# First layer of a two-layer trunk: head sums in column groups, roots spread from 32 rows, the mixing bias as a table, and halves of the u products between the small products

## The reference

```python
def chunk_gating(u, va, w_s, b_s):               # 8 groups of 64 columns, chunks of 128 tokens
    vc = va.reshape(b, t // CHUNK, CHUNK, A_GROUPS, A_GROUP_DIM)
    s = jnp.einsum('gpq,bnqgc->bnpgc', w_s, vc) + b_s.T[None, None, :, :, None]
    return u * s.reshape(b, t, A_WIDTH)

def even_project(h, w_in, q_gain, k_gain):
    u, va, q, k, v = jnp.split(h @ w_in, list(EV_SPLITS), axis=-1)     # 512, 512, 512, 128, 128 columns
    q = rms_norm(q.reshape(b, t, B_KV_HEADS, B_GROUP, HEAD_DIM), q_gain)   # per head of 64
    k = rms_norm(k.reshape(b, t, B_KV_HEADS, HEAD_DIM), k_gain)
# latent tokens: q = axial_rope(q, ...), k = axial_rope(k, ...), then block attention;
# out = concatenate([u * s, attention]) @ w_out; a mixture of experts follows; layer 2 likewise
```

## Time and profile before

| | |
|---|---|
| time, median of 3 runs | 1390.81 us (1388.46 to 1392.39) |
| the profiled execution | 1387.17 us, its span in the trace 1385.0 us |
| mean granted TensorE clock | 0.949 |
| PE busy | 1263.4 us, 91% of the span |
| DVE, ACT, POOL busy | 870.2, 705.5, 235.9 us |
| DMA | 324.98 MB, mean 235 GB/s |

### The profile page before, as it was taken

How to read it: one execution, slowest core, us unless ns; L and a number is a source line. 1 busy time by engine, 2 the same in 40 slices (tenths; PEclk the granted TensorE clock), 3 DMA queues, 4 the chain that set the end, 5 groups by cost and what they waited for, 6 DMA issues and landing times.

```text
span 1385.0 us, 18165 instructions
## 1 busy us (share of the span) xinstructions
PE 1263.4 (91%) x7550; PEld 911.6 (66%) x7550; DVE 870.2 (63%) x1013; ACT 705.5 (51%) x819; POOL 235.9 (17%) x133
## 2 busy tenths in 40 slices
PE   5999988899399999999789998999984999999997
PEld 2897856788266666666469984667872666666662
DVE  5613546423678888888385252553344899999994
ACT  3531146611467777777343124554123777776772
POOL 3100000011302222211030000000124033333330
PEclk9997899999699999999899999899996999999996
DMA  9710182042799999999883222002419999999974
GB/s 364 247 63 31 33 277 104 1 153 92 275 369 357 384 379 380 385 391 397 290 276 103 95 68 72 1 1 92 153 41 381 379 376 377 385 383 382 393 294 161
DMA packets 100472, 324.98 MB, mean 235 GB/s; under 512 B 6720, under 2 KB 30495, under 8 KB 84007
## 3 DMA queue, kind: packets, MB, share of 16 engines
q1 hardware_dynamic: 89376, 290.88, 55.7%
q0 software_dynamic: 8400, 27.58, 7.7%
q10 hardware_dynamic: 2614, 5.35, 1.0%
HBM read 300.29 MB, written 23.50 MB: 234 GB/s over the span
## 4 chain that ended last, share of the span: by engine, by line
PE 74%; DMA 8%; ACT 7%; DVE 6%; POOL 2%; issue 1%; SPq 0%; ACTq 0%; POOLq 0%; DVEq 0%
PE psum L944 71%; ACT arena L1814 4%; DVE arena L2270 2%; DMA stage<-in_moe_w_up 2%; DVE w_lo L2000 2%; DMA h_hi<-h_dram,arena 1%; POOL arena L891 1%; PE psum L1464 1%; DMA stage<-in_moe_w_gate 1%; DMA h_dram<-arena 1%; DMA stage<-in_w_mod 1%; DMA arena<-in_x_sample 1%; DMA arena<-in_od_w_in 1%; ACT arena L1581 1%; ACT w_hi L1890 1%
## 5 line engine op out<-in xcount | busy, mean ns | idle before, releaser
L944 PE MATMUL psum<-w_hi,h_hi 128*80 128x512 f32 (+1 forms) x848 | 330.4, 390 | 8.4 <-DVE w_lo L2000 5.0
L2000 DVE TENSOR_TENSOR w_lo<-stage,w_hi 128x2048 fp32r<-128x2048 f32 (+1 forms) x122 | 275.5, 2270 | 99.5 <-ACT w_hi L1594 59.5
L944 PE MATMUL psum<-w_lo,h_hi 128*80 128x512 f32 (+1 forms) x848 | 326.0, 384 | 0.0
L944 PE MATMUL psum<-w_hi,h_lo 128*80 128x512 f32 (+1 forms) x848 | 325.7, 384 | 0.0
L1890 ACT ACTIVATE w_hi<-stage 128x2048 fp32r<-128x2048 f32 x100 | 190.6, 1915 | 60.2 <-PE psum L944 37.0
L944 PE MATMUL psum<-h_hi,w_hi 128*128 128x320 f32 x672 | 212.4, 316 | 2.0 <-DVE h_lo L2047 2.0
L944 PE MATMUL psum<-h_lo,w_hi 128*128 128x320 f32 x672 | 209.7, 312 | 0.0
L944 PE MATMUL psum<-h_hi,w_lo 128*128 128x320 f32 x672 | 209.6, 312 | 0.0
L909 POOL DMA_INDIRECT acc_dram<-arena x31 | 120.2, 3878 | 413.0 <-ACT arena L1922 227.8
L2000 DVE TENSOR_TENSOR w_lo<-arena,w_hi 128x2048 fp32r<-128x2048 f32 x73 | 166.7, 2288 | 31.0 <-ACT w_hi L1890 28.2
L944 PEld LDWEIGHTS psum<-w_hi,h_hi 128*80 128x80 f32 (+1 forms) x848 | 129.9, 153 | 82.5 <-issue 13.7
(11 more groups left out here) (275 smaller groups left out, 1289.8 us busy)
## 6 DMA issues: line engine op xcount, KB each, us to landing
stage<-in_w_mod SPq DMA_DIRECT2D x46, 1024.0 KB, 9.0
stage<-in_moe_w_up SPq DMA_DIRECT2D x36, 1024.0 KB, 15.7
stage<-in_moe_w_down SPq DMA_DIRECT2D x34, 1024.0 KB, 15.0
stage<-in_moe_w_gate SPq DMA_DIRECT2D x30, 1024.0 KB, 15.2
arena<-in_moe_w_gate SPq DMA_DIRECT2D x29, 1024.0 KB, 16.2
arena<-in_moe_w_up SPq DMA_DIRECT2D x23, 1024.0 KB, 15.4
arena<-in_moe_w_down SPq DMA_DIRECT2D x19, 1024.0 KB, 15.5
xT<-in_moe_w_down SPq DMA_DIRECT2D x11, 1024.0 KB, 19.5
```

The costliest lines, as they stand in the source:

```text
L944: return pe.matmul(o, w, x, start=first, stop=last, skip_group_check=True)
L2000: return nc.vector.tensor_tensor(dst, src, hi.bitcast(F32), ALU.subtract)
```

## The change

On TensorE:

- `head_sums` uses two tables of 128x32 in place of five of 128x10. Tile k and q 0, q 1, q 2 write output rows 0 to 31, 32 to 63, 64 to 95, 96 to 127; q 3 adds to the rows of k with the second table. The roots then lie on all 128 partitions, two of each 32 in use. The result has new banks, 6 and 7, which hold `va 0` before, and a new product group `s bias` stands ahead of it.
- A spread reads the 32 rows of its group, table and roots, in place of 10.
- The mixing bias is made once: four products of 128x128 from the 8 rows, brought by ScalarE to a table `s_bias`. The four 8-row products of 512 columns and the four of 128 columns go. VectorE adds the table where it copied the mixing out.
- Each u product but the last is cut in two halves of 24 products along the inner axis, and the spreads, mixings and pair turns stand between the halves. `u 0` starts behind the second spread. The mixing of the context comes first of the mixings.
- The rows of modulation chunk 4 come ahead of `u 3`, those of chunk 5 behind it, and both transposes after that.

On VectorE and ScalarE the order follows: the low part of `out 0` is made after the second scaling, that of `out 1` after the third mixing; ScalarE splits the second u piece behind the roots, and `out 1` ahead of the swapped keys (which now wait for the last mixing), and brings over the rows of chunk 4 before the four gated tiles. The scratch tile of the rotation and the tables lie elsewhere, and banks are given by name in `plan_psum`.

```diff
+HEAD_GROUP, SECOND_IN_GROUP = {4: 0, 0: 1, 1: 2, 2: 3, 3: 0}, 3
...
+            one("v lat", "act"), one("v ctx", "act"), one("cache k", "act"), one("s bias", "act", in_order=False)
...
+            for name, banks in ((("qk spread", 4), (0, 1)), (("qk spread", 0), (2, 3)), (("qk spread", 1), (0, 1)), (("qk spread", 2), (2, 3)),
...
+        pick_ = small[:, 256:320]
+        pick = pick_.rearrange("p (m r) -> p m r", m=2)
+        pick_rows = arena[:, 5248:5248 + 2 * P]
+        head_var, head_root = rstd, sq[0]
+        s_bias = v3(arena, T, 4, P)
...
-                    mm(bank(name, 0)[0:10, :], pick[:, m, :], head_sq[m][:, LAT], m == 0, m == 4)
-                    ins = mm(bank(name, 1)[0:10, 0:NC], pick[:, m, :], head_sq[m][:, CTX], m == 0, m == 4)
+                    own = slice(32 * HEAD_GROUP[m], 32 * HEAD_GROUP[m] + 32)
+                    w = pick[:, int(m == SECOND_IN_GROUP), :]
+                    mm(bank(name, 0)[own, :], w, head_sq[m][:, LAT], m < 4, m != SECOND_IN_GROUP)
+                    ins = mm(bank(name, 1)[own, 0:NC], w, head_sq[m][:, CTX], m < 4, m != SECOND_IN_GROUP)
                     ins.then_inc(sq_used if m < 4 else psum_full, 1)
...
-                    for m in range(5):
-                        ins = pe.transpose(pair("pick rows", 10, 5 * P)[:, P * m:P * m + P], pick[:, m, :], ident)
-                    ins.then_inc(psum_full, 1)
+                    for g in range(4):
+                        mm(bank("pick rows")[32 * g:32 * g + 32, 0:P], pick[:, 0, :], ident, True, True)
+                    mm(bank("pick rows", 1)[0:32, 0:P], pick[:, 1, :], ident, True, True).then_inc(psum_full, 1)
...
+                    pe.wait_ge(sel_in, 16)
+                    begin("s bias")
+                    for g in range(4):
+                        ins = mm(bank("s bias")[:, P * g:P * g + P], sel[:, g, :], bs, True, True)
+                    ins.then_inc(psum_full, 1)
                     head_sums("qk norm")
...
+                    def spread_root(m):
+
+                        name, g = ("qk spread", m), 32 * HEAD_GROUP[m]
+                        at = P * int(m == SECOND_IN_GROUP)
                         begin(name)
+                        mm(bank(name, 0), pick_rows[g:g + 32, at:at + P], head_root[g:g + 32, LAT], True, True)
...
+                    def mix_latents(g):
+
                         begin(("s", g))
-                        b_rows = bs.rearrange("p (o q) -> p o q", o=1).to_broadcast([8, 4, P])
-                        mm(bank(("s", g)).rearrange("p (o q) -> p o q", o=4), sel[:, g, :], b_rows, True, False)
                         for t in range(4):
                             for j in range(2):
                                 ins = mm(bank(("s", g))[64 * j:64 * j + 64, P * t:P * t + P],
-                                         va[:, t, P * g + 64 * j:P * g + 64 * j + 64], ws_tile(2 * g + j), False, t == 3)
+                                         va[:, t, P * g + 64 * j:P * g + 64 * j + 64], ws_tile(2 * g + j), True, True)
...
+                    def project_half(m, part_of_k):
+
+                        hi, lo = weights(("u", m // 2))
+                        name, c = ("u", m), P * (m % 2)
+                        if part_of_k == 0:
+                            begin(name)
+                        for k in range(4 * part_of_k, 4 * part_of_k + 4):
+                            w = (hi[:, k, c:c + P], lo[:, k, c:c + P])
+                            for half in range(2):
+                                tk = slice(HT * half, HT * half + HT)
+                                ins = passes(bank(name, half)[:, 0:HT], w, (h_hi[:, k, tk], h_lo[:, k, tk]), k == 0, k == KD - 1)
+                        if part_of_k == 1:
+                            ins.then_inc(psum_full, 1)
+
+                    spread_root(4)
+                    spread_root(0)
+                    project_half(0, 0)
+                    spread_root(1)
+                    spread_root(2)
+                    project_half(0, 1)
+                    spread_root(3)
+                    emptied(pe, ("va", 1, 2))
+                    emptied(pe, "wsT1")
+                    mix_context()
+                    mix_latents(0)
+                    pe.wait_ge(cs_in, 16)
+                    turn_pairs(4)
+                    project_half(1, 0)
+                    turn_pairs(0)
+                    mix_latents(1)
+                    project_half(1, 1)
+                    turn_pairs(1)
+                    mix_latents(2)
+                    project_half(2, 0)
+                    turn_pairs(2)
+                    mix_latents(3)
+                    project_half(2, 1)
+                    turn_pairs(3)
                     begin("new k")
                     pe.transpose(bank("new k")[:, 0:P], kT[:, P + NL:KEYS], ident).then_inc(psum_full, 1)
-                    project(("u", 0), [("u", 1)], at=(P,))
-                    project(("u", 1), [("u", 2), ("u", 3)])
-                    modulation("qk")
+                    mod_rows(MOD_AT["qk"][0])
+                    project_half(3, 0)
+                    project_half(3, 1)
+                    mod_rows(MOD_AT["qk"][1])
+                    turn_mod(MOD_AT["qk"][0])
+                    turn_mod(MOD_AT["qk"][1])
                     pe.wait_ge(k_swapped, 2)
                     pe.wait_ge(roped, 5)
...
-                    split(keys[6])
+                    evacuate("s bias", s_bias.rearrange("p g q -> p (g q)"), bank("s bias"))
                     emptied(act, "qk norm")
                     nc.scalar.activation(head_root, head_var, ACT.Ln).then_inc(log_done, 1)
                     logs[0] += 1
                     act.wait_ge(log_done, logs[0])
                     nc.scalar.activation(head_root, head_root, ACT.Exp, scale=-0.5).then_inc(root_done, 1)
+                    split(keys[6])
                     evacuate_va(1)
                     split((L, "out", 0))
+                    split((L, "out", 1))
                     act.wait_ge(roped, 1)
                     emptied(act, "cache k")
+                    filled(act, ("s", 3))
                     nc.scalar.activation(kX[64:128, :], kT[0:64, :], ACT.Copy).then_inc(k_swapped, 1)
                     nc.scalar.activation(kX[0:64, :], kT[64:128, :], ACT.Copy).then_inc(k_swapped, 1)
-                    split((L, "out", 1))
+                    modulation("qk", slice(0, 1))
...
+                    modulation("qk", slice(1, 2))
...
+                    def mixed_latents(g):
+
                         filled(dve, ("s", g))
-                        freeing(nc.vector.tensor_copy(gated[:, g, LAT], bank(("s", g))))
-                    filled(dve, ("s", "ctx"))
-                    freeing(nc.vector.tensor_copy(gated[:, :, CTX], bank(("s", "ctx")).rearrange("p (m n) -> p m n", m=4)))
-                    emptied(dve, ("s", "ctx"))
+                        bias = s_bias[:, g, :].rearrange("p (o q) -> p o q", o=1).to_broadcast([P, 4, P])
+                        freeing(nc.vector.tensor_tensor(gated[:, g, LAT].rearrange("p (t q) -> p t q", t=4),
+                                                        bank(("s", g)).rearrange("p (t q) -> p t q", t=4), bias, ALU.add))
...
                     def gate(m):
                         filled(dve, ("u", m))
+                        emptied(dve, ("s", m))
                         freeing(nc.vector.tensor_tensor(two(gated[:, m, :]), halves(("u", m)), two(gated[:, m, :]), ALU.mult))
...
+                    scale_heads(4)
+                    scale_heads(0)
+                    split((L, "out", 0))
+                    scale_heads(1)
+                    scale_heads(2)
+                    scale_heads(3)
+                    emptied(dve, "s bias")
+                    filled(dve, ("s", "ctx"))
+                    freeing(nc.vector.tensor_tensor(gated[:, :, CTX], bank(("s", "ctx")).rearrange("p (m n) -> p m n", m=4), s_bias, ALU.add))
+                    mixed_latents(0)
+                    gate(0)
+                    dve.wait_ge(cs_in, 16)
+                    rotate_heads(4)
+                    rotate_heads(0)
+                    mixed_latents(1)
+                    gate(1)
+                    rotate_heads(1)
+                    mixed_latents(2)
+                    split((L, "out", 1))
+                    rotate_heads(2)
+                    mixed_latents(3)
+                    gate(2)
+                    rotate_heads(3)
                     filled(dve, "new k")
                     freeing(nc.vector.tensor_copy(small[:, P:2 * P], bank("new k")[:, 0:P]))
-                    gate(1)
```

More of the change, by code:

```diff
@@ L205, in plan_psum @@
                 one(("va", 0, b), "act", in_order=False)
-            one("v lat", "act"), one("v ctx", "act"), one("cache k", "act")
+            one("v lat", "act"), one("v ctx", "act"), one("cache k", "act"), one("s bias", "act", in_order=False)
             for b in range(3):
                 p.frees(("va", 0, b))
+            p.frees("s bias")
```

(39 more changed lines are left out.)

41 lines of the change are left out of this document (12 added, 29 removed), and 3 rows, old and new, of the table chunks.

## The result

The changed kernel takes 1370.03 us (median of 4 runs, 1363.36 to 1375.29) against 1389.65 for the kernel before in the same comparison (4 runs, 1388.46 to 1392.39). The ratio is 0.9845, with a 95% interval from 0.9815 to 0.9875: 1.6% faster, 17 to 26 us. 1371.8 was forecast. The profiled execution took 1372.22 us, its span 1370.4; mean granted clock 0.958.

A forecast was written before the change was run, and what follows sets the result against it. TensorE bounds the kernel, with 74% of the chain of waits. Bias and head sums -1.6, wait +0.2, stage -16.3 and tail -1.7 sum to -19.4: 1390.81 becomes 1371.4, put at 1371.8 us, range 1366 to 1379.

The forecast's parts named there:

- The clock: First spread to first scores: PEclk stays 1.00 with 32-row spreads, two at a time, u products between.
- Head sums: Head sums before `va 1`: four column groups run side by side, 2.2 us in place of 5.5.
- The rival of 4.8: Head sums run one after another in a strict queue, 4.8 us; total change -16.8, time 1374.0; chance 0.35.
- Wait ahead of them: Before the head sums: their banks wait for ScalarE to empty `va 0`, start 99.72 becomes 101.4, +1.7 us.
- Wait ahead of the first spread: Behind `va 1`: the first spread waits for ScalarE's second evacuation, ending near 120.0, +0.2 us.
- Stage: First spread to the end of `u 3`: at full clock 45.9 us against 62.2, -16.3 (-14.9 with dear shape switches).
- the terms other than the spreads: Within `u 3`'s stretch: u products 28.1, mixings 5.25, pair turns and key transpose 4.3, chunk 4 rows 1.7, shape switches 1.2.
- Tail: Behind `u 3` to the first scores: second evacuation and transposes leave the path, scores at 186.7 against 188.45, -1.7 us.
- Covers: VectorE's low part of `out 1` has 5 us margin; chunk 5's last piece lands by 41, wanted at 45.
- Sum: Whole change up to the first scores: -1.6 + 0.2 - 16.3 - 1.7 = -19.4 us.
- the rivals: Strict-queue head sums 1374.0 (0.35); part-stage clock fall 1378.4 (0.12); time unchanged 1390.8 (0.04); slower attention 1429 (0.03).
- the partial fall: Clock falls behind each of the first two spread pairs, 3.5 us each; total -12.4, 1378.4; chance 0.12.

The follow-up runs named there:

- e5_flat_rows4: e1_flat with spreads that read 4 rows in place of 32, bias still a table; stage 45.67 us, 6.8 of it at half clock.
- e1_flat: The changed kernel with the stage in the order of before, without interleaving; stage 42.64 us, median 1370.45, ratio to the kernel before 0.986.
- e9_table_only: The kernel before with only the mixing bias made as a table; median 1377.93 against 1390.85, ratio 0.9916, stage 45.93 us.
- e6: e5_flat_rows4 with the four latent 8-row bias products back ahead of their mixings; stage 58.33 us, 23.9 of it at half clock.
- e3_bias: The changed kernel with the four latent bias products (8 rows, 512 columns) back in the mixings; stage 48.86 us, none at half clock.
- e11_bias_again: e3_bias unchanged, in another execution; stage again 48.86 us, none at half clock.
- e8_flat_banks: e1_flat with other banks for head sums, `va 1` and spreads, and table products behind the head sums; stage 42.67 us, median 1369.76, ratio 0.9859.
- e7_flat_bias: e1_flat with the four latent bias products back; stage 55.36 us, 17.1 of it at half clock.
- e10_flat_bias_again: e7_flat_bias unchanged, in another execution; stage 47.44 us, none at half clock.

## Why the prediction was right, step by step

**The clock.** Right in the main: 1.00 from the first spread to the first scores. But the prediction blamed the rows of the spreads and credited 32 rows with u products between. The runs split it. Spreads of 4 or 10 rows start a fall, which costs 3.0 by itself (e5_flat_rows4 against e1_flat; e9_table_only has the same 6.8 us at half clock, so about 3.4). The bias products keep it down for some 17 to 20 us more (23.9 against 6.8 in e6 and e5, 27.3 against 6.8 in the kernel before and e9) and make up the larger part: 12.7 us lie between e5 and e6, of which 4.4 to 4.8 is their work. The prediction put the table into its sum as work alone, so it didn't foresee that the table alone takes away most of the time at half clock. Its forecast of 1.00 didn't need that: 32 rows with u products between kept 1.00 with the bias products as well (e3_bias, e11_bias_again). In the order of before, 32 rows with the bias products had a fall of 17 us in one of two executions. The interleaving is a second remedy for the same ill. With the table it costs 1.9; with products it had 48.9 twice where the order of before gave 47.4 or 55.4.

**Head sums.** Forecast 2.2, measured 2.3: four column groups side by side, although each has two products in a row. The rival of 4.8 is out. The first passes of four tiles start within 0.05 us of each other at 100.79, ahead of the first tile's 128-column product (101.65), which stands before three of them in the program. The Trainium skill's rule of a strict queue (TensorE: Matmul & The Clock Gate, "The mechanism") does not hold here: the trace decides, and by the rule the part would have been some 2.5 us longer (4.8, as the prediction estimated it).

**Wait ahead of them.** Forecast +1.7, measured +1.9. **Wait ahead of the first spread.** Forecast +0.2, measured +0.5: ScalarE needed until 118.05 for the second evacuation.

**Stage.** Forecast -16.3, measured -17.4. The step that was mis-sized is the spreads: 5.33 us reckoned one after another, 4.0 measured, because spreads of different row groups overlap. I had seen that for column groups and not carried it over to rows. The rest of the stage came as summed: 40.7 from start to start, where the terms other than the spreads add up to 40.6. The 1.9 between e1_flat and the changed kernel, which has the same products, splits into 0.45 for spreads (four overlap there, two here) and 1.4 for the other products, behind thirteen more changes of shape: 0.11 each, near the 1.2 of the sum. The Trainium skill's sentence that a change of tiling mode drains the array (TensorEngine Tiling (Array Packing), "Key Properties") fits that sign.

**Tail.** Forecast -1.7, measured -1.9. **Covers.** VectorE's low part of `out 1` and chunk 5's last piece were in time, as reckoned; TensorE has no gap in the stage.

**Sum.** Forecast -19.4 to the first scores, measured -20.0, and -19.6 in the medians. The errors cancel in part, by luck: the stage came out 1.1 better than forecast, the two waits 0.5 worse. None of the rivals came; the partial fall came only where 4 rows were put back, at 1.5 us rather than 7.

## What to carry to other kernels

When a clock fall spans a run of small products, take each kind out by itself before reordering: here a table that replaces eight products of 8 rows gave 14.9 of 20 us, and the long reordering, with the table in place, cost 1.9. Small products that sit in one row or column group in turn are worth spreading over the groups: five took the time of two. And a saving of 3 us in a 1370 us kernel has to be shown in the trace of its stage when the rest moves by 12 us from one execution to the next.

## What the runs showed of the hardware that was not expected

- Products of 512 and then 128 columns, each pair in its own group, run side by side: 20 passes of head sums in four column groups in 2.3 us (5.5 in one group), 16 passes of spreads in four row groups in 1.65 (e1_flat) to 2.1 (e8_flat_banks), where one after another four spreads take 4.3.
- The clock fell with TensorE without a gap in its work and came back under mixings of 128 rows and 64 columns alone (e5, e9: 6.8 us at 1.2 GHz in all), while the same mixings with 8-row products between them left it at 1.2 GHz for 17 to 27 us.
- The head sums, 128 rows by 10 columns, 5.5 us at a stretch, had no fall behind them in e9_table_only either, as in the kernel before. Products of few rows did. That the rows count and the columns don't is read from these two cases and wasn't tried by itself.
- The fall can depend on the moment: one kernel (e7_flat_bias, e10_flat_bias_again) had 17 us at half clock in one execution of the stage and none in the next.
